# A two-block transformer kernel on one core: three mixer operand pairs packed into one buffer, a 24-slot weight store refilled in another order, and the last gain multiplies on GpSimd

## The chip, the core and the metric

The kernel runs on one core of one Trainium2 chip. A core has five engines with instruction streams of their own: TensorE (PE, matrix products), VectorE (DVE), ScalarE (ACT), GpSimd (POOL) and SyncE (SP), which here does little but start DMA transfers. Data stand in SBUF, products in PSUM, weights in HBM, from which 16 DMA engines fetch them. The metric is the device time of one execution in microseconds (us); lower is better.

## What is computed

A sequence of 256 tokens of width 1024 goes through two blocks of two layers each, all in float32. The first block has a mixer and a mixture of experts in each layer; the second has attention and a convolutional feed-forward network. The parts around the change are these:

```python
# first block, for layer 0 (convolution mixer) and layer 1 (recurrent mixer)
x = layer_norm(ALPHA * x + mixer(x), ln1_g[layer], ln1_b[layer])
f = moe(x, w_router, b_router, moe_w1[layer], moe_w3[layer], moe_w2[layer])
x = layer_norm(ALPHA * x + f, ln2_g[layer], ln2_b[layer])

# both mixers end in a projection
return jnp.einsum("bse,ed->bsd", concatenated_or_gated, w_out)

# each of the 16 experts of a layer
hb = jax.nn.silu(xb @ w1[e]) * (xb @ w3[e])
return hb @ w2[e]

# the end of the second block
x = x + conv_ffn(h, w_up, conv_w, conv_b, w_down)
return rms_norm(x, final_norm_g)        # x * rsqrt(mean(x*x) + eps) * g
```

## The kernel before

**Weights as a stream.** All weights are cut into chunks of 128 x 2048 floats (1 MB). `STREAM` lists them: the input projection of a mixer, its output projection (`ew_out` in layer 0, `ow_out` in layer 1, four chunks each), then 192 expert chunks for a layer (`moe0`, `moe1`; four each of w1, w3 and w2 for each of 16 experts). `sync_load` (L366) starts the loads from SP in the order of `LOAD_ORDER`, which for the first two experts interleaves them: w1 of both, w3 of expert 0, w3 of expert 1, then w2 of both. One load is one DMA of 1 MB, or of 2 MB where `_load_size` gives 2. In this text load 0 is the first expert chunk of a layer, and a 2 MB load has the number of its first chunk.

**Slots.** A chunk lands in one of 24 slots: 0 to 11 are the tile `ring`; 12 to 16 lie in `F` (work space of the mixers and experts), 17 to 20 are the four parts of `early`, 21 and 22 the two halves of `ZX`, and 23 a last part of `F`, used once for each layer. Before it starts a load SP waits until the chunk that was in the slot is used (`released`), and for the first 24 expert loads also until other data are gone from it (`extra_free`). SP works in order, so one wait holds all loads behind it. `FIRST_SLOTS` gives slots to some of the first 24 loads, the rest get the slot that is free first. `GROUPS` names the pairs that a 2 MB load may take; slots 16 and 23 are in no pair.

**The four parts of `early`** have another life in the projections. A dense product is made of three passes on numbers split in a high and a low part: the weights' parts stand in `wh` and `wl` (slots 17 and 18; four pieces of 512 columns, refilled by `scalar_split` on ACT and `vector_split` on DVE), the left operand's in `xh` and `xl` (slots 19 and 20). The output projection of a mixer has four operand pairs q = 0 to 3 (`operand`, L553): pair 0 stands in `F`, pairs 1 to 3 in parts of `xh` and of `xl`. Each takes four weight pieces; `w_used` counts the pieces that PE has used.

**The experts.** `tensor_first_pair` runs experts 0 and 1 together, `moe_tensor` the others one after another. Eight matmul records belong to one chunk (L1431 for w1 of the first pair, L1231 elsewhere). After the last of a chunk `expert_chunk` is raised and its slot is free. From load 128 of a layer on only slots 0 to 11 and 21 are filled, since the others get other work.

**The end.** The last stage `down1` adds its product to `X` (`vector_residual`, L768, four parts: token half h, column half d), takes the squares' sums on ACT (`scalar_rms`, L784), adds them (`vector_rms_sum`, L789), raises to the power -0.5 on POOL (`pool_rstd`, L575), and multiplies by the gain `G` (`gain` in `vector_finish`, L2978, DVE). The product is scaled by the row's factor, on ACT for d = 0 (`scalar_finish`, L3000) and on DVE for d = 1 (`scale`, L2982), and stored by four DMAs (`sync_store`, L3008). The squares are written to `Z`, where the gain's product also goes, so `gain` waits for `square`.

Of the kernel before, what the change touches and what calls it, by code (L numbers as in the profile page):

```python
# [11 lines left out]
ALU = mybir.AluOpType  # L12
# [77 lines left out]
def f32(ap):  # L90
# [26 lines left out]
F_SLOTS, SPLIT_SLOTS, Z_SLOT, XT_SLOT, ONCE_SLOT = range(12, 17), range(17, 21), 21, 22, 23  # L117
FIRST_SLOTS = ([12, 13, 14, 15, XT_SLOT] + [None] * 11 + [16, None, ONCE_SLOT, None, 17, 18, 19, 20],
               [None] * 8 + [16, XT_SLOT, 15, None, None, 14, None, 13, None, 12, ONCE_SLOT, None, 17, 18, 19, 20])
LOAD_ORDER = list(range(len(KIND)))  # L120
# [6 lines left out]
def _load_size(i):  # L127

    return 2 if 40 <= i < 180 else 1

# [88 lines left out]
class Kernel:  # L219
# [311 lines left out]
    def tensor_out_last(self, stage, p, nk):  # L531

        pe, PS = self.pe, self.PS
        pe.wait_ge(self.at("g_lo", stage, nk // 2 - 1))
        for m in range(2):
            x = slice(m * 128, m * 128 + 128)
            for d in range(2):
                for kk in range(2):
# [3 lines left out]
                    pe.wait_ge(self.at("w_lo", n))  # L542
                    t = self.three(PS[:, 2 * m + d, :], (self.xh[:, k % 8, x], self.xl[:, k % 8, x]), (h, l),
                                   False, kk == 1)
# [233 lines left out]
    def scalar_rms(self, stage, src_stage, h):  # L778

        act = self.act  # L780
        for d in range(2):
            c = slice(d * 512, d * 512 + 512)
            act.wait_ge(self.at("resid", src_stage, h, d) if src_stage else self.at("x_final", h))
            act.e.activation(self.Z[:, h, c], self.X[:, h, c], ACT.Square, scale=1.0 / 32,  # L784
                             accum_out=self.sm[:, 430 + 2 * h + d:431 + 2 * h + d]).then_inc(*self.up("square", stage, h, d))
# [201 lines left out]
    def even_scalar(self):  # L987
# [45 lines left out]
        for h in range(2):  # L1033
            for c in (2 * h, 2 * h + 1):
                act.wait_ge(at("ev_scaled", h), at("ev_var"), at("ev_consts", "bh"))
                act.e.activation(v["sq"][:, c, :], v["acc"][:, c, :], ACT.Tanh, scale=v["gh"][:, c:c + 1],
                                 bias=v["bh"][:, c:c + 1]).then_inc(*up("ev_tanh", c))
            self.scalar_split_x("ew_out", 2 + h, self.GT[:, 4 + 2 * h:6 + 2 * h, :], at("ev_gated", 2 * h + 1))
        for n in range(8, 16):
# [964 lines left out]
    def odd_scalar(self):  # L2004
# [404 lines left out]
    def out_scalar(self, stage, p, nk, ready, primed=0):  # L2409
# [14 lines left out]
        self.scalar_rms(stage, stage, 0)
        self.scalar_finish(0)
        self.scalar_rms(stage, stage, 1)
        self.scalar_finish(1)

# [541 lines left out]
    def vector_finish(self, p, nk):  # L2970

        dve, at, up = self.dve, self.at, self.up
        G = self.F[:, 12288:13312]

        def gain(h, d):
            c = slice(d * 512, d * 512 + 512)
            dve.wait_ge((self.s_row, 48), at("resid", "down1", h, d), at("square", "down1", h, d))
            dve.e.tensor_tensor(self.Z[:, h, c], self.X[:, h, c], G[:, c], ALU.mult).then_inc(*up("y_gain", h, d))  # L2978

        def scale(h):  # L2980
            dve.wait_ge(at("rstd", ("down1", h)), at("y_gain", h, 1))
# [3 lines left out]
        self.vector_residual("down1", p, nk, 0, 1.0, self.X)
        self.vector_rms_sum("down1", 0)
        gain(0, 0)
        gain(0, 1)
        self.vector_residual("down1", p, nk, 1, 1.0, self.X, halves=(0,))
        scale(0)  # L2990
        self.vector_residual("down1", p, nk, 1, 1.0, self.X, halves=(1,))
        gain(1, 0)
        self.vector_rms_sum("down1", 1)
        gain(1, 1)
        scale(1)

# [166 lines left out]
```

## Time and profile before

| | us |
|---|---|
| median of 3 runs | 1774.01 |
| lowest and highest | 1773.5, 1775.23 |
| the profiled execution | 1775.5 |
| its span, first to last instruction | 1774.2 |
| PE busy, share of the span | 1709.8, 96% |
| DMA traffic, mean over the span | 307 GB/s |

The page cuts the span in 40 slices of 44 us and gives the DMA rate of each. A window table gives busy time by engine for a stretch, the granted clock, then the DMA engines' share (1.00: all 16 busy) and GB/s. A timeline gives start, duration, engine, line and operation, with like neighbours merged ("x4"); a bracket at its end is the idle time before and what ended it. The view of DMA issues gives for each load its size and the us from issue to landing. The loads have one line, L379, so they are told apart by time.

### The profile page before, as it was taken

The page shows a single profiled execution, that of the slowest core. Times are in us where ns is not written, and L with a number is a line of the kernel's source. Part 1 is how long each engine was busy: PE and PEld are TensorE (multiplying, and loading weights), DVE is VectorE, ACT ScalarE, POOL GpSimd, SP SyncE. Part 2 cuts the span into 40 slices and gives each one's busy share as a digit, 9 for nine tenths or more (in the row PEclk, how much of TensorE's full clock was granted, in tenths as well). Part 3 has the DMA queues.
Part 4 walks back from the last instruction along what each step waited for, and adds up shares of the span by engine and source line. Part 5 has one row for each costly group of instructions (what it writes and reads, how often), then busy time and mean ns, then how long its engine had stood idle before and what let it go on. Part 6 is the DMA issues. An engine that isn't in the chain of part 4 may idle for free.

```text
span 1774.2 us, 23971 instructions
## 1 busy us (share of the span) xinstructions
PE 1709.8 (96%) x9996; PEld 1116.9 (63%) x9996; DVE 791.5 (45%) x1522; ACT 625.2 (35%) x1201; POOL 122.4 (7%) x145
## 2 busy tenths in 40 slices
PE   9999999999989989999999989999999999999998
PEld 8974344433334974444343333887999898789986
DVE  6961111111103782111111012866888677668875
ACT  5541111000002661100000002666666564756664
POOL 0000000000000000000000000131111001401100
PEclk9999999999999999999999999999999999999999
DMA  9769999999999789999999999434555544335550
GB/s 387 314 232 381 387 428 428 428 430 426 426 426 419 284 320 395 423 429 429 429 426 429 425 426 419 174 129 143 177 180 190 190 167 149 137 131 178 179 190 24
DMA packets 55971, 544.88 MB, mean 307 GB/s; under 512 B 6320, under 2 KB 6320, under 8 KB 8368
## 3 DMA queue, kind: packets, MB, share of 16 engines
q1 hardware_dynamic: 55440, 542.14, 75.8%
q8 instruction: 82, 1.34, 0.3%
q10 hardware_dynamic: 416, 1.13, 0.2%
q14 instruction: 33, 0.27, 0.0%
HBM read 542.19 MB, written 1.05 MB: 306 GB/s over the span
## 4 chain that ended last, share of the span: by engine, by line
PE 71%; DMA 16%; DVE 7%; ACT 3%; issue 1%; POOL 1%; SPq 0%; ACTq 0%; DVEq 0%
PE PS L1231 24%; DMA ring<-in_w 16%; PE PS L421 12%; PE PS L423 11%; PE PS L422 11%; PE PS L1213 2%; PE PS L1285 2%; DVE wl L404 2%; PE PS L1431 2%; PE PS L950 1%; PE PS L1247 1%; ACT wh L398 1%; PE PS L1299 1%; PE PS L1404 0%; DVE sm L593 0%
## 5 line engine op out<-in xcount | busy, mean ns | idle before, releaser
L1231 PE MATMUL PS<-ring,F 128*64 128x512 f32 x1992 | 447.4, 598 | 27.5 <-DMA ring<-in_w 23.4
L404 DVE TENSOR_TENSOR wl<-ring,wh 128x512 fp32r<-128x512 f32 x504 | 362.4, 737 | 167.4 <-ACT wh L398 164.9
L398 ACT ACTIVATE wh<-ring 128x512 fp32r<-128x512 f32 x504 | 314.5, 630 | 270.0 <-PE PS L423 251.9
L1231 PEld LDWEIGHTS PS<-ring,F 128*64 128x64 f32 x1992 | 142.3, 138 | 312.0 <-issue 273.6
L421 PE MATMUL PS<-xh,wl 128*128 128x256 f32 x1144 | 329.8, 288 | 2.7 <-DVE wl L404 2.6
L422 PE MATMUL PS<-xl,wh 128*128 128x256 f32 x1144 | 323.6, 283 | 0.0
L423 PE MATMUL PS<-xh,wh 128*128 128x256 f32 x1144 | 323.5, 283 | 0.0
L421 PEld LDWEIGHTS PS<-xh,wl 128*128 128x128 f32 x1144 | 219.2, 192 | 5.8 <-DVE wl L404 2.7
L422 PEld LDWEIGHTS PS<-xl,wh 128*128 128x128 f32 x1144 | 219.3, 192 | 0.7
L423 PEld LDWEIGHTS PS<-xh,wh 128*128 128x128 f32 x1144 | 219.3, 192 | 0.0
L421 PE MATMUL PS<-wh,xl 128*128 128x512 f32 x352 | 142.6, 405 | 6.5 <-DVE xl L566 3.4
L423 PE MATMUL PS<-wh,xh 128*128 128x512 f32 x352 | 137.5, 391 | 0.0
L422 PE MATMUL PS<-wl,xh 128*128 128x512 f32 x352 | 137.3, 390 | 0.0
L1758 DVE COPY F<-PS 64x512 f32<-64x512 f32 x26 | 18.1, 695 | 223.1 <-PE PS L1231 223.1
L1733 DVE SCALAR_TENSOR_TENSOR F<-F,PS 128x512 f32<-128x512 f32 x28 | 19.2, 687 | 203.9 <-ACT F L1548 203.9
L1738 DVE SCALAR_TENSOR_TENSOR F<-F,PS 128x512 f32<-128x512 f32 x28 | 19.2, 687 | 183.1 <-PE PS L1231 183.1
L1231 PE MATMUL PS<-F 128*64 128x512 f32 x384 | 87.1, 594 | 0.4 <-DMA F<-in_w 0.4
L1548 ACT ACTIVATE F<-PS 128x512 f32<-128x512 f32 x28 | 16.7, 597 | 189.3 <-PE PS L1231 189.3
L421 PEld LDWEIGHTS PS<-wh,xl 128*128 128x128 f32 x352 | 66.1, 188 | 26.8 <-DVE xl L566 6.4
L1566 ACT ACTIVATE F<-PS 64x512 f32<-64x512 f32 x26 | 15.3, 590 | 187.6 <-PE PS L1231 187.6
L2643 DVE SCALAR_TENSOR_TENSOR F<-PS,cols,F 128x254 f32<-128x254 f32 (+1 forms) x176 | 76.3, 474 | 1.5
L423 PEld LDWEIGHTS PS<-wh,xh 128*128 128x128 f32 x352 | 66.1, 188 | 14.4
(422 smaller groups left out, 1907.5 us busy)
## 6 DMA issues: line engine op xcount, KB each, us to landing
ring<-in_w SPq DMA_DIRECT2D x100, 2048.0 KB, 25.6
ring<-in_w SPq DMA_DIRECT2D x65, 1024.0 KB, 11.7
ring<-in_ffn_up SPq DMA_DIRECT2D x44, 1024.0 KB, 4.9
early<-in_w SPq DMA_DIRECT2D x16, 2048.0 KB, 26.6
F<-in_w SPq DMA_DIRECT2D x16, 2048.0 KB, 27.9
ring<-in_ffn_down SPq DMA_DIRECT2D x22, 1024.0 KB, 4.9
F<-in_w SPq DMA_DIRECT2D x20, 1024.0 KB, 9.3
ZX<-in_w SPq DMA_DIRECT2D x8, 2048.0 KB, 28.0
```

What stands on the lines that cost most here:

```text
L398: act.e.activation(self.wh[:, p % NPIECE, :], self.piece_source(p), ACT.Copy).then_inc(*self.up("w_hi", p))
L404: dve.e.tensor_tensor(self.wl[:, p % NPIECE, :], self.piece_source(p), f32(self.wh[:, p % NPIECE, :]), ALU.subtract).then_inc(*self.up("w_ ...
L421: e.matmul(out, left[1], right[0], start=first, stop=False)
L422: e.matmul(out, left[0], right[1], start=False, stop=False)
L423: return e.matmul(out, left[0], right[0], start=False, stop=last)
L1213: t = pe.e.matmul(self.PS[:, 6 + half, k4 * 128:k4 * 128 + 128], self.X[:, h, k * 128:k * 128 + 128], v["S"][:, h, :], start=(h == 0), sto ...
L1231: t = pe.e.matmul(PS[64 * half:64 * half + 64, bank, :], lhs(k), weights[:, a:a + 512], start=(k == 0), stop=(k == 7))
L1285: t = pe.e.matmul(self.PS[:, b, :], v["Gt"][:, h, d, :], v["Y"][d], start=(q == 0), stop=False)
L1431: t = pe.e.matmul(PS[64 * half:64 * half + 64, self.first_bank(ex, 0), :], xg[:, k, ex * 64:ex * 64 + 64], weights[:, a:a + 512], start=(k ...
L1733: e.scalar_tensor_tensor(out=self.silu(ex), in0=self.silu(ex), scalar=1.0, in1=PS[:, 4, :], op0=ALU.add, op1=ALU.mult).then_inc(*up("silu" ...
L1738: e.scalar_tensor_tensor(out=v["hh"], in0=self.silu(ex), scalar=0.5, in1=PS[:, 5, :], op0=ALU.mult, op1=ALU.mult).then_inc(*up("hidden", l ...
L2643: t = dve.e.scalar_tensor_tensor(out=dst[:, j, s:256], in0=ps[:, j, 0:256 - s], scalar=cw[:, k, 2 - s:3 - s], in1=dst[:, j, s:256], op0=AL ...
```

## The change

1. **Operand pairs of the mixer outputs.** For `ew_out` and `ow_out` the pairs 1, 2 and 3 all stand in `xl`: high part and low part of a pair side by side, pair 2 in the upper half, pairs 1 and 3 in the lower half. Pair 3 is written after PE has used pair 1 (`w_used`, piece 7). `xh` has no reader after the last piece of the input projection.
2. **One more chunk.** Slot 19 (`xh`) is filled as load 15 in layer 0 and load 12 in layer 1, after that last piece, where it was load 22. The loads that stood there move back by one.
3. **2 MB loads begin with load 44**, not 40. Loads 39 to 43 are single ones, and the pairs of slots for all later loads come in another order.
4. **The end.** Squares are written to a free part of `F`. Three of four gain multiplies are on POOL (`pool_gain`), around `pool_rstd`; DVE keeps the one for h = 1, d = 1. DVE has both residual parts of h = 1 ahead of it, and both scales last. ACT makes all four squares ahead of both `scalar_finish`.

```diff
-FIRST_SLOTS = ([12, 13, 14, 15, XT_SLOT] + [None] * 11 + [16, None, ONCE_SLOT, None, 17, 18, 19, 20],
-               [None] * 8 + [16, XT_SLOT, 15, None, None, 14, None, 13, None, 12, ONCE_SLOT, None, 17, 18, 19, 20])
+FIRST_SLOTS = ([12, 13, 14, 15, XT_SLOT] + [None] * 10 + [19, None, 16, None, ONCE_SLOT, None, 17, 18, 20],
+               [None] * 8 + [16, XT_SLOT, 15, None, 19, None, 14, None, 13, None, 12, ONCE_SLOT, None, 17, 18, 20])
-    return 2 if 40 <= i < 180 else 1
+    return 2 if 44 <= i < 180 else 1
 def extra_free(self, n):
+        if slot == SPLIT_SLOTS[2]:
+            return [self.at("w_used", PIECES[mixer] - 1)]
 def operand(self, stage, q):
+        if stage in MIXER_OUT and q:
+            a = 4 * ((q + 1) % 2)
+            return self.xl[:, a:a + 2, :], self.xl[:, a + 2:a + 4, :]
 def scalar_rms(self, stage, src_stage, h):
+            squares = self.F[:, 8704 + 512 * d:9216 + 512 * d] if stage == "down1" else self.Z[:, h, c]
 def odd_scalar(self):
-        self.scalar_split_x("ow_out", 3, GT[:, 6:8, :], at("od_join", 3))
+        self.scalar_split_x("ow_out", 3, GT[:, 6:8, :], at("od_join", 3), at("w_used", p + 7))
 def out_scalar(...):
+        for h in range(2):
+            self.scalar_rms(stage, stage, h)
+        for h in range(2):
+            self.scalar_finish(h)
 def ffn_pool(self, layer):
+        if layer:
+            for d in range(2):
+                self.pool_gain(0, d)
+        self.pool_rstd(0, (f"down{layer}", 0))
+        if layer:
+            self.pool_gain(1, 0)
+        self.pool_rstd(1, (f"down{layer}", 1))
 def vector_finish(self, p, nk):
+        self.vector_residual("down1", p, nk, 0, 1.0, self.X)
+        self.vector_rms_sum("down1", 0)
+        self.vector_residual("down1", p, nk, 1, 1.0, self.X)
+        dve.wait_ge((self.s_row, 48), at("resid", "down1", 1, 1))
+        dve.e.tensor_tensor(self.Z[:, 1, 512:1024], self.X[:, 1, 512:1024], self.last_gain()[:, 512:1024], ALU.mult
+                            ).then_inc(*up("y_gain_last"))
+        self.vector_rms_sum("down1", 1)
+        for h in range(2):
+            dve.wait_ge(at("rstd", ("down1", h)), at("y_gain_last") if h else at("y_gain", 0, 1))
+            dve.e.tensor_scalar(self.Z[:, h, 512:1024], self.Z[:, h, 512:1024], self.sm[:, 500 + h:501 + h], None,
+                                ALU.mult).then_inc(*up("y_ready1", h))
```

SP, expert loads of layer 0 before, from load 24 to load 49 (128x2048 is 1 MB, 128x4096 is 2 MB; `early` is slots 17 to 20, `F` slots 12 to 16, `ZX` slots 21 and 22):

```order
L379 DMA F<-in_w 128x2048 [waits s_expert_chunk] x4
L379 DMA ZX<-in_w 128x2048 [waits s_expert_chunk]
L379 DMA ring<-in_w 128x2048 [waits s_expert_chunk] x11
L379 DMA early<-in_w 128x4096 [waits s_expert_chunk] x2
L379 DMA F<-in_w 128x4096 [waits s_expert_chunk] x2
L379 DMA ZX<-in_w 128x4096 [waits s_expert_chunk]
```

The same loads now:

```order
L382 DMA F<-in_w 128x2048 [waits s_expert_chunk] x4
L382 DMA ZX<-in_w 128x2048 [waits s_expert_chunk]
L382 DMA ring<-in_w 128x2048 [waits s_expert_chunk] x10
L382 DMA early<-in_w 128x2048 [waits s_expert_chunk]
L382 DMA ring<-in_w 128x2048 [waits s_expert_chunk]
L382 DMA F<-in_w 128x2048 [waits s_expert_chunk]
L382 DMA ZX<-in_w 128x2048 [waits s_expert_chunk]
L382 DMA ring<-in_w 128x2048 [waits s_expert_chunk]
L382 DMA early<-in_w 128x4096 [waits s_expert_chunk]
L382 DMA F<-in_w 128x4096 [waits s_expert_chunk] x2
```

Load 40 was a pair in slots 17 and 18, which hold w2 of expert 1; it is now one chunk in slot 11, which holds the second w2 chunk of expert 0. Loads 41, 42 and 43 follow in slots 16, 21 and 0.

DVE, the end of the program before:

```order
L768 TENSOR_TENSOR X<-X,PS 128x512 [waits s_half_done] x2
L789 TENSOR_SCALAR sm<-sm 128x1 [waits s_square]
L2978 TENSOR_TENSOR ZX<-X,F 128x512 [waits s_resid,s_row]
L2978 TENSOR_TENSOR ZX<-X,F 128x512 [waits s_resid]
L768 TENSOR_TENSOR X<-X,PS 128x512 [waits s_w_used]
L2982 TENSOR_SCALAR ZX<-ZX,sm 128x512 [waits s_y_gain,s_norm_scale]
L768 TENSOR_TENSOR X<-X,PS 128x512 [waits s_w_used]
L2978 TENSOR_TENSOR ZX<-X,F 128x512 [waits s_square,s_resid]
L789 TENSOR_SCALAR sm<-sm 128x1 [waits s_square]
L2978 TENSOR_TENSOR ZX<-X,F 128x512 [waits s_resid]
L2982 TENSOR_SCALAR ZX<-ZX,sm 128x512 [waits s_y_gain,s_norm_scale]
```

and now:

```order
L775 TENSOR_TENSOR X<-X,PS 128x512 [waits s_half_done] x2
L797 TENSOR_SCALAR sm<-sm 128x1 [waits s_square]
L775 TENSOR_TENSOR X<-X,PS 128x512 [waits s_w_used] x2
L2991 TENSOR_TENSOR ZX<-X,F 128x512 [waits s_resid,s_row]
L797 TENSOR_SCALAR sm<-sm 128x1 [waits s_square]
L2996 TENSOR_SCALAR ZX<-ZX,sm 128x512 [waits s_y_gain,s_norm_scale]
L2996 TENSOR_SCALAR ZX<-ZX,sm 128x512 [waits s_y_gain_last,s_norm_scale]
```

Three multiplies and one scale no longer stand ahead of the last residual part and the last sum. On POOL, whose program had ended in two `pool_rstd` in a row, it is now:

```order
L3007 TENSOR_TENSOR ZX<-X,F 128x512 [waits s_resid,s_row]
L3007 TENSOR_TENSOR ZX<-X,F 128x512 [waits s_resid]
L582 TENSOR_TENSOR sm<-sm,mhalf 128x1 [waits s_norm_stats]
L3007 TENSOR_TENSOR ZX<-X,F 128x512 [waits s_resid]
L582 TENSOR_TENSOR sm<-sm,mhalf 128x1 [waits s_norm_stats]
```

so that each power stands behind multiplies.

## Rows read from the trace of the kernel before

**Rows 1.** The page: DMA rate in 40 slices of 44 us.
```profile
GB/s 387 314 232 381 387 428 428 428 430 426 426 426 419 284 320 395 423 429 429 429 426 429 425 426 419 174 129 143 177 180 190 190 167 149 137 131 178 179 190 24
```
**Rows 2.** Windows in layer 0: engines' busy us, clock, DMA share, GB/s.
```profile
150.00:170.00 20.00, 20.00 (x100) 7.73 (x97) 3.42 (x8) 1.68 (x3) 0.00 (x0) 1.00 1.01 422
170.00:180.00 10.00, 10.00 (x66) 5.93 (x64) 1.39 (x2) 1.68 (x3) 0.00 (x0) 1.00 0.76 315
180.00:190.00 10.00, 10.00 (x50) 3.33 (x48) 0.69 (x1) 0.59 (x1) 0.00 (x0) 1.00 0.84 339
210.00:350.00 140.00, 140.00 (x686) 55.79 (x683) 19.13 (x47) 15.35 (x27) 0.00 (x0) 1.00 1.01 428
350.00:548.00 198.00, 183.87 (x849) 69.81 (x847) 18.96 (x37) 16.35 (x28) 0.00 (x0) 0.99 1.01 426
```
**Rows 3.** Timeline of SP: loads 24 to 27, 36 to 39, 40 and 42; layer 1's 24.
```profile
134.97 6.80 SPq L379 DMA_DIRECT2D F<-in_w  x4
...
161.25 6.67 SPq L379 DMA_DIRECT2D ring<-in_w  x4
180.57 3.76 SPq L379 DMA_DIRECT2D early<-in_w  x2
...
675.95 0.33 SPq L379 DMA_DIRECT2D ZX<-in_w  x1
```
**Rows 4.** DMA issues at 99.7, 167.6, 180.6, 197.7, 746.8 us: size, us to landing.
```profile
ring<-in_w SPq DMA_DIRECT2D x1, 1024.0 KB, 4.8
...
ring<-in_w SPq DMA_DIRECT2D x1, 1024.0 KB, 13.0
...
early<-in_w SPq DMA_DIRECT2D x1, 2048.0 KB, 8.6
...
ring<-in_w SPq DMA_DIRECT2D x1, 2048.0 KB, 20.7
...
ZX<-in_w SPq DMA_DIRECT2D x1, 2048.0 KB, 9.0
```
**Rows 5.** Timeline of PE: last reads of xh, first expert products, later ones.
```profile
86.97 0.28 PE L423 MATMUL PS<-xh,wh 128*128 128x256 f32 x1
...
133.00 3.65 PE L1431 MATMUL PS<-F 128*64 128x512 f32 x16
...
167.38 1.89 PE L1231 MATMUL PS<-F 128*64 128x512 f32 x8
...
176.83 7.09 PE L1231 MATMUL PS<-early,F 128*64 128x512 f32 x32
...
202.09 5.37 PE L1231 MATMUL PS<-ring,F 128*64 128x512 f32 x24
...
635.05 0.28 PE L423 MATMUL PS<-xh,wh 128*128 128x256 f32 x1
```
**Rows 6.** Waits of PE from 350 to 562 us: total, times, longest.
```profile
PE PS L1231 <- DMA ring<-in_w: 12.3, 11, 2.5
```
**Rows 7.** Timeline of the last 12 us: DVE, PE, ACT.
```profile
1762.93 0.69 DVE L768 TENSOR_TENSOR X<-X,PS 128x512 f32<-128x512 f32 x1
...
1766.58 0.39 PE L423 MATMUL PS<-wh,xh 128*128 128x512 f32 x1
...
1768.09 0.68 DVE L768 TENSOR_TENSOR X<-X,PS 128x512 f32<-128x512 f32 x1
...
1769.56 0.21 DVE L789 TENSOR_SCALAR sm<-sm 128x1 f32<-128x1 f32 x1 [0.19 <-ACT ZX L784]
...
1770.82 0.72 ACT L3000 ACTIVATE ZX<-ZX,sm 128x512 f32<-128x512 f32 x1 [1.29 <-POOL sm L575]
```
**Rows 8.** A POOL multiply and the DVE beside it; all 18 powers (min/median/max ns).
```profile
1258.77 1.29 POOL L2684 TENSOR_TENSOR F<-F 128x512 f32<-128x512 f32 x1
...
1258.88 1.73 DVE L404 TENSOR_TENSOR wl<-ring,wh 128x512 fp32r<-128x512 f32 x1 [0.68 <-ACT wh L398]
...
L575 POOL TENSOR_TENSOR sm<-sm,mhalf x18: 537/548/932, 119.1 to 1769.9; 128x1 f32<-128x1 f32 x18
```

More of the change, by code:

```diff
@@ L22 @@
 PE_TAPS = 11
+MIXER_OUT = ("ew_out", "ow_out")
 ROUTED = ("ew_out", "ow_out")
@@ L533, in tensor_out_last @@
         pe, PS = self.pe, self.PS
+        xh, xl = self.operand(stage, nk // 2 - 1)
         pe.wait_ge(self.at("g_lo", stage, nk // 2 - 1))
@@ L542, in tensor_out_last @@
                     pe.wait_ge(self.at("w_lo", n))
-                    t = self.three(PS[:, 2 * m + d, :], (self.xh[:, k % 8, x], self.xl[:, k % 8, x]), (h, l),
+                    t = self.three(PS[:, 2 * m + d, :], (xh[:, kk, x], xl[:, kk, x]), (h, l),
                                    False, kk == 1)
@@ L783, in scalar_rms @@
             act.wait_ge(self.at("resid", src_stage, h, d) if src_stage else self.at("x_final", h))
-            act.e.activation(self.Z[:, h, c], self.X[:, h, c], ACT.Square, scale=1.0 / 32,
+            squares = self.F[:, 8704 + 512 * d:9216 + 512 * d] if stage == "down1" else self.Z[:, h, c]
+            act.e.activation(squares, self.X[:, h, c], ACT.Square, scale=1.0 / 32,
                              accum_out=self.sm[:, 430 + 2 * h + d:431 + 2 * h + d]).then_inc(*self.up("square", stage, h, d))
@@ L1037, in even_scalar @@
                                  bias=v["bh"][:, c:c + 1]).then_inc(*up("ev_tanh", c))
-            self.scalar_split_x("ew_out", 2 + h, self.GT[:, 4 + 2 * h:6 + 2 * h, :], at("ev_gated", 2 * h + 1))
+            self.scalar_split_x("ew_out", 2 + h, self.GT[:, 4 + 2 * h:6 + 2 * h, :], at("ev_gated", 2 * h + 1),
+                                *([at("w_used", p + 7)] if h else []))
         for n in range(8, 16):
@@ L2423, in out_scalar @@
             return
[L2424 to L2427, printed above, removed]
+        for h in range(2):
+            self.scalar_rms(stage, stage, h)
+        for h in range(2):
+            self.scalar_finish(h)
     def scalar_split_before(self, p, end):
@@ L2684, in ffn_pool @@
             pool.e.tensor_tensor(acc[i % 2][0], acc[i % 2][0], th[i % 2], ALU.mult).then_inc(*up("gated_unit", layer, i))
-        for h in range(2):
-            self.pool_rstd(h, (f"down{layer}", h))
+        if layer:
[5 more added lines that the diff above has]
+        self.pool_rstd(1, (f"down{layer}", 1))
     def dilated_views(self):
@@ L2972, in vector_finish, with last_gain, pool_gain @@
         dve, at, up = self.dve, self.at, self.up
[L2973 to L2981, printed above, removed]
+        self.vector_residual("down1", p, nk, 0, 1.0, self.X)
[7 more added lines that the diff above has]
+            dve.wait_ge(at("rstd", ("down1", h)), at("y_gain_last") if h else at("y_gain", 0, 1))
             dve.e.tensor_scalar(self.Z[:, h, 512:1024], self.Z[:, h, 512:1024], self.sm[:, 500 + h:501 + h], None,
                                 ALU.mult).then_inc(*up("y_ready1", h))
[L2985 to L2995, printed above, removed]
+    def last_gain(self):
+        return self.F[:, 12288:13312]
+    def pool_gain(self, h, d):
+        c = slice(d * 512, d * 512 + 512)
+        self.pool.wait_ge((self.s_row, 48), self.at("resid", "down1", h, d))
+        self.pool.e.tensor_tensor(self.Z[:, h, c], self.X[:, h, c], self.last_gain()[:, c], ALU.mult).then_inc(
+            *self.up("y_gain", h, d))
     def scalar_finish(self, h):
```

## The prediction, made before the changed kernel ran

> **What bounds the kernel now.** I read the page's DMA rates first [rows 1]. Two plateaus near 426 to 430 GB/s stand out, slices 6 to 13 and 17 to 25, one for each layer's experts. The windows say what is full there: from 210 to 350 us PE is busy all the time and the DMA engines too, from 350 to 548 us the DMA engines are full and PE is busy for 183.87 of 198 us [rows 2]. So PE starts ahead of the stream with full slots, and the stream, which is slower, has caught it up by about 350 us; from there PE waits for landings, 11 times and 12.3 us in all [rows 6]. The end of a layer's experts is therefore the end of its stream: bytes by 426 GB/s, plus each us in which the DMA engines had nothing to do. A load that lands earlier is worth something only if no later load has to wait for a slot all the same. That is the question to ask of edits 2 and 3.
>
> Next I looked for the last such hole in layer 0. The DMA share falls to 0.76 and 0.84 between 170 and 190 us, with 1.01 ahead of it and 1.01 behind [rows 2]. SP shows why: it starts loads 36 to 39 from 161.25 to 167.9 us, then nothing until load 40 at 180.57 [rows 3]. Load 40 is a pair in slots 17 and 18, and PE reads these only from 176.83 us on, 1.77 us for a chunk (7.09 us for 32 records, four chunks) [rows 5], so both are free at 180.5. Load 39 landed at 167.6 + 13.0 = 180.6, so the slowest DMA engine too ran dry, and load 40 landed at 180.6 + 8.6 = 189.2 [rows 4]. A full stream brings 2.10 MB in 4.90 us at 428 GB/s [rows 2]; the hole costs 8.6 - 4.9 = 3.7 us.
>
> **Edit 3 (2 MB loads from load 44).** Load 40 is now one chunk in slot 11, whose chunk (expert 0's second w2) PE has used when its 8 records that begin at 167.38 us end, at about 169.3 [rows 5]. Loads 41 and 42 follow at 1.7 us each, 43 after the first chunk of the group at 176.83, by 178.8. All of them are issued before load 39 has landed, so the queue doesn't run dry. Singles take 1.05 MB / 422 GB/s = 2.48 us [rows 2], so loads 40 to 43 end at 180.6 + 9.9 = 190.5, where before they ended at 189.2 + 4.9 = 194.1. **Gain in layer 0: 3.6 us.**
>
> Does a later load take it back? The tightest is load 52: now in slots 4 and 5, which hold expert 2's first two w2 chunks, used at 202.09 + 2 x 1.8 = 205.7 [rows 5]. On an empty queue it would land 8.6 us after that, at 214.3. The stream reaches it at 190.5 + 5 x 4.9 = 215.0. So it is not late, by 0.7 us. Before, load 52 landed at 197.7 + 20.7 = 218.4 [rows 4]. The gain therefore is 3.4 to 3.6 by the stream and cannot be over 218.4 - 214.3 = 4.1. It passes on to the end of the layer, as PE has 12.3 us of waits to give up [rows 6], and to all that follows.
>
> In layer 1 the same hole isn't there: the DMA rate stays full from slice 17 on, that is from 710 us [rows 1]. There, load 52 needs slots 21 and 22 both before and now, freed at the same PE chunk; it was issued at 746.8 and landed 9.0 us later, at 755.8, where an empty queue would give 755.4 [rows 4]. So layer 1 can gain no more than 0.4 us from edits 2 and 3 together. I take 0.
>
> The windows of singles and doubles, 422 and 428 GB/s [rows 2], show no part of a transfer that is paid in line beyond 0.03 us. A rule of the Trainium skill speaks against edit 3: "DMA: Bandwidth & Descriptors", section "Anatomy of one DMA — SWDGE (gpsimd) path", gives each DMA a fixed part of about 2.0 us beside its bytes. By that page, an estimate with two more transfers for each layer, paid in line, is 8 us more; the trace doesn't agree as long as others are queued (rival D).
>
> **Edits 1 and 2 (xh free early, one more chunk).** `xh` has its last reader at 86.97 us in layer 0 and 635.05 in layer 1 [rows 5]. The new load 15 of layer 0 goes out after load 14 and before the one at 99.7, which was landed 4.8 us later, so it fills an idle DMA engine; it is behind no late wait. It saves nothing: there are 24 slots before and after. Load 24 waits for the first expert chunk to be used, at 134.97 [rows 3] as PE's first products begin at 133.00 [rows 5], and by then all 24 loads are in anyway, one of them 2.5 us sooner. Layer 1 has the same gate at 675.95 [rows 3]. **0 us**, with the caps above as bounds. Pair 3's new wait for `w_used` piece 7 costs nothing on ACT: ACT's own weight splits ahead of it wait for that same piece. DVE's split waits for ACT only. PE's matmul count is the same.
>
> **Edit 4 (the end).** Before, the second residual part of h = 1 began at 1768.09, though PE's last matmul ended at 1766.58 + 0.39 = 1766.97 [rows 7]: DVE was held by multiplies. Now it begins at 1767.0, 1.09 us sooner. From the residual to the last sum it takes 1768.09 to 1769.56, from the sum to the scales 1.26 us [rows 7].
> POOL: first residual done at 1763.62 [rows 7], two multiplies of 1.29 us with 0.1 between [rows 8] to 1766.4, the power, whose median is 0.55 us and most 0.93 [rows 8], to 1767.0, then the multiply for h = 1 to 1768.35.
> DVE: its one multiply comes at 1767.7, amid that. A DVE operation with two SBUF inputs that began 0.11 us after a POOL multiply took 1.73 us and ended 0.55 us after it [rows 8]. So DVE's ends at 1768.9, and the sum begins there, not at 1768.5. With 1.26 us the scales begin at 1770.1, with the power at its short 0.55 at 1769.7. Before: 1770.82. Gain 0.7 to 1.1, I take **0.9 us**. The stores behind keep their spacing. Upper bound 1.5, if DVE isn't held and the power is short (1.09 + 0.38). Lower bound: if each of the three POOL multiplies lost as much to DVE as DVE lost to POOL, 1.73 - 0.69 = 1.04, the second power would end at 1768.35 + 3.1 + 0.55 = 1772.0, a loss of 1.2.
>
> **Sum.** The profiled execution took 1775.5 with a span of 1774.2; the median is 1774.01, and I subtract from that: 1774.0 - 3.6 - 0 - 0.9 = **1769.5 us**. The span should be 1769.7.
>
> **Rivals.**
> A. The extra chunk is carried through as a head start in both layers, 2.5 us each, because the slowest DMA engine binds and it alone was still busy when load 24 came. For: that the load whose bytes take 2.5 us landed 4.8 us after issue [rows 4] leaves room for a start that overlaps better. Against: the caps of load 52, 4.1 and 0.4 us. Time: 1769.5 - 5.0 = 1764.5.
> B. The hole only moves. With the pairs in another order the queue runs dry at load 52 or later, and layer 0 gains nothing. For: a margin of 0.7 us, on a latency seen once for a pair on an empty queue. Against: as soon as it holds, later loads are issued further ahead, since PE is the faster. Time: 1774.0 - 0.9 = 1773.1.
> C. Slower: restart. The DMA engines now stand idle for 2.5 us longer ahead of load 24, in both layers, all 16 of them. If a restart from fully dry costs as the one at 180 did (3.7 us for hole and start together), once more in each layer, it is 1774.0 - 4.5 + 7.4 = 1776.9. It decides if the landing of loads 24 and 25 is later than before by over 2.3 us a layer. Against: single loads on a dry queue landed in 4.8 us [rows 4], 2.3 over their bytes, the same before and now.
> D. Slower: the fixed part is paid in line. By rows it is 4.8 - 2.5 = 2.3 us for a single; two more transfers a layer make 9.2 us: 1778.7. Against: 422 beside 428 GB/s.
>
> **How the numbers follow.** Forecast 0.75, A 0.07, B 0.11, C 0.05, D 0.02. The forecast's own range takes the caps (4.1 + 0.4 + 1.5 = 6.0: 1768.0) and on the other side the losing end (3.4 - 1.2 = 2.2: 1771.8). With B at 1773.1 in it and some scatter of the runs (1773.5 to 1775.2) on the low side, 1767.0 to 1773.2 holds over 0.8. A measurement tells about 0.2% or 3.5 us from no change, so faster means under 1770.5. The forecast lies there in about 5 of 6 of its cases, 0.63, with A 0.70; the rest of it and B make 0.23 the same; C and D 0.07 slower.
>
> **What would show it.** Right: DMA share near 1.0 from 140 us to the end of layer 0's experts, load 40 landing at about 183 and load 52 at 215; the last landing and all stages behind 3.6 us earlier; the first expert products at 131.8 us as before, layer 1's expert stretch as long as before; in the last 12 us a DVE multiply of 1.2 us or more, and scales that begin 2.7 to 3.1 us after PE's last matmul, where it was 3.85. Wrong: a hole near 205 us (B), loads 24 and 25 later (C), landings of singles over 2.6 us apart (D), load 24 itself issued earlier or layer 1 shorter by over 0.4 us (A).

## The result and the profile after

| | us |
|---|---|
| before, median of 7 runs | 1774.23 |
| after, median of 7 runs | 1768.88 (1768.28 to 1770.26) |
| ratio | 0.997, 95% interval 0.9961 to 0.9979 |
| the profiled execution after, its span | 1770.26, 1769.0 |

The changed kernel is 5.35 us faster, where 4.5 were forecast, and 1769.5 was forecast for 1768.88. The profiled execution is the slowest of the seven. The loads' line L379 is L382 now, L423 is L426, and L1231 is L1240.

The page of the changed kernel has its two plateaus where they were [rows 1], and the windows of layer 0 (columns as in [rows 2]) show the hole at 180 us filled:

```profile
GB/s 389 315 238 378 420 429 427 427 429 427 425 424 420 275 345 375 420 430 427 429 427 427 423 426 420 182 125 143 180 180 189 191 167 147 140 132 170 188 189 26
```
```profile
170.00:180.00 10.00, 10.00 (x66) 5.88 (x64) 1.39 (x2) 1.68 (x3) 0.00 (x0) 1.00 1.01 419
180.00:190.00 10.00, 10.00 (x50) 3.43 (x48) 0.69 (x1) 0.59 (x1) 0.00 (x0) 1.00 1.03 432
203.00:206.00 3.00, 3.00 (x16) 1.01 (x14) 0.00 (x0) 0.00 (x0) 0.00 (x0) 1.00 0.99 426
206.00:209.00 3.00, 3.00 (x16) 1.00 (x14) 0.12 (x1) 0.12 (x1) 0.00 (x0) 1.00 0.95 311
210.00:350.00 140.00, 140.00 (x687) 56.03 (x684) 19.12 (x47) 15.35 (x27) 0.00 (x0) 1.00 1.01 428
```

315 and 339 GB/s have become 419 and 432. There is a new, smaller dip, 311 GB/s from 206 to 209 us. SP's timeline of the changed kernel, layer 0 (loads 24 to 27, 29 to 38, 40, 43, 44, then 50 and 52) and load 24 of layer 1:

```profile
134.63 6.80 SPq L382 DMA_DIRECT2D F<-in_w  x4
...
145.86 20.00 SPq L382 DMA_DIRECT2D ring<-in_w  x10
...
168.97 0.33 SPq L382 DMA_DIRECT2D ring<-in_w  x1
...
178.47 0.33 SPq L382 DMA_DIRECT2D ring<-in_w  x1
181.95 0.33 SPq L382 DMA_DIRECT2D early<-in_w  x1
...
197.40 8.42 SPq L382 DMA_DIRECT2D ring<-in_w  x2
...
672.72 0.33 SPq L382 DMA_DIRECT2D ZX<-in_w  x1
```

DMA issues of the changed kernel at 89.8 (the extra chunk), 169.0 (load 40), 205.5 (load 52) and 743.5 us (load 52 of layer 1), size and us to landing:

```profile
early<-in_w SPq DMA_DIRECT2D x1, 1024.0 KB, 6.9
...
ring<-in_w SPq DMA_DIRECT2D x1, 1024.0 KB, 12.6
...
ring<-in_w SPq DMA_DIRECT2D x1, 2048.0 KB, 8.6
...
ZX<-in_w SPq DMA_DIRECT2D x1, 2048.0 KB, 8.9
```

Load 40 landed at 169.0 + 12.6 = 181.6 (183 forecast), load 52 at 205.5 + 8.6 = 214.1 (215.0 forecast, 218.4 before).

The last 12 us of the changed kernel, timelines of PE, DVE, POOL and ACT:

```profile
1762.55 0.39 PE L426 MATMUL PS<-wh,xh 128*128 128x512 f32 x1
...
1762.98 0.69 DVE L775 TENSOR_TENSOR X<-X,PS 128x512 f32<-128x512 f32 x1 [0.43 <-PE PS L426]
1763.77 0.84 DVE L2991 TENSOR_TENSOR ZX<-X,F 128x512 f32<-128x512 f32 x1
1764.53 0.20 DVE L797 TENSOR_SCALAR sm<-sm 128x1 f32<-128x1 f32 x1
...
1764.23 0.19 ACT L792 ACTIVATION_READ_ACCUMULATOR F<-X 128x1 f32 x1
...
1759.73 2.59 POOL L3007 TENSOR_TENSOR ZX<-X,F 128x512 f32<-128x512 f32 x2 [56.46 <-DVE X L775]
1762.27 0.55 POOL L582 TENSOR_TENSOR sm<-sm,mhalf 128x1 f32<-128x1 f32 x1
1762.79 1.27 POOL L3007 TENSOR_TENSOR ZX<-X,F 128x512 f32<-128x512 f32 x1
1764.81 0.72 POOL L582 TENSOR_TENSOR sm<-sm,mhalf 128x1 f32<-128x1 f32 x1 [0.75 <-DVE sm L797]
...
1765.57 0.72 ACT L3013 ACTIVATE ZX<-ZX,sm 128x512 f32<-128x512 f32 x1 [0.54 <-POOL sm L582]
```

The last scales begin 1765.57 - 1762.94 = 2.63 us after the end of PE's last matmul, where it was 3.85 [rows 7].

**Where the 5.2 us of span went.** The same instruction in both traces, by [rows 3, 7] and the rows above: load 24 of layer 0 is issued 0.34 us earlier (chance: nothing ahead of it is quicker by design), load 24 of layer 1 3.23 earlier, the last matmul 4.03, the last scales 5.25. So 2.9 us fell in layer 0's stretch, 0.8 between layer 1's load 24 and the last matmul, and 1.2 in the end. The 0.8 is not the stream's: layer 1's last load landed only 2.8 us earlier than before, so that in this execution its stream took 0.5 us longer (419.8 us from the issue of load 24 to the last landing, for 419.3; the other traces with the extra chunk and 2 MB loads have 418.0 to 419.1), and 1.3 us fell between that landing and the last matmul. This part is a slow stretch of PE in the trace of before (last section).

### The profile page after: what moved, and what is told of

Its sections match the earlier page's. It is cut to its first block, busy times and chain, and to the rows that moved or that the text cites. A ratio compares the mean times of both kernels' runs of the same rounds, so it can differ in the third digit from the quotient of the medians.

```text
span 1769.0 us, 23968 instructions
## 1 busy us (share of the span) xinstructions
PE 1709.5 (97%) x9996; PEld 1116.6 (63%) x9996; DVE 789.8 (45%) x1519; ACT 625.1 (35%) x1201; POOL 125.6 (7%) x148
## 4 chain that ended last, share of the span: by engine, by line
PE 69%; DMA 18%; DVE 7%; ACT 3%; issue 1%; POOL 1%; SPq 0%; ACTq 0%; DVEq 0%
PE PS L1240 22%; DMA ring<-in_w 18%; PE PS L424 12%; PE PS L426 11%; PE PS L425 11%; PE PS L1222 2%; DVE wl L407 2%; PE PS L1440 2%; PE PS L1294 2%; PE PS L958 1%; PE PS L1256 1%; ACT wh L401 1%; PE PS L1308 1%; PE PS L1413 1%; DVE sm L600 0%
## 5 line engine op out<-in xcount | busy, mean ns | idle before, releaser
L1240 PE MATMUL PS<-ring,F 128*64 128x512 f32 x1984 | 446.4, 597 | 25.4 <-DMA ring<-in_w 20.0
L1240 PEld LDWEIGHTS PS<-ring,F 128*64 128x64 f32 x1984 | 140.6, 137 | 308.1 <-issue 268.3
L426 PE MATMUL PS<-xh,wh 128*128 128x256 f32 x1144 | 323.5, 283 | 0.0
L425 PEld LDWEIGHTS PS<-xl,wh 128*128 128x128 f32 x1144 | 219.3, 192 | 0.6
L426 PEld LDWEIGHTS PS<-xh,wh 128*128 128x128 f32 x1144 | 219.3, 192 | 0.0
L426 PE MATMUL PS<-wh,xh 128*128 128x512 f32 x304 | 118.7, 391 | 0.0
L425 PE MATMUL PS<-wl,xh 128*128 128x512 f32 x304 | 118.6, 390 | 0.0
L1240 PE MATMUL PS<-F 128*64 128x512 f32 x384 | 87.1, 593 | 0.0
L1240 PE MATMUL PS<-early,F 128*64 128x512 f32 x336 | 76.1, 594 | 0.0
```

The costliest lines, as they stand in the source:

```text
L425: e.matmul(out, left[0], right[1], start=False, stop=False)
L426: return e.matmul(out, left[0], right[0], start=False, stop=last)
L1240: t = pe.e.matmul(PS[64 * half:64 * half + 64, bank, :], lhs(k), weights[:, a:a + 512], start=(k == 0), stop=(k == 7))
```

## The experiments

All are timed beside the kernel before, whose median was 1774.2 to 1774.3 each time. For the stream I read one mark from each profile: the time from the issue of load 24, which is where PE has used the layer's first chunk, to the landing of load 100. It leaves out what happened ahead of the layer.

| kernel | extra chunk | 2 MB from | time, us | layer 0 mark | layer 1 mark |
|---|---|---|---|---|---|
| before | no | 40 | 1774.2 | 201.0 | 198.1 |
| end4 | no | 40 | 1772.90 | 201.1 | 197.5 |
| load44 | no | 44 | 1770.73 | 196.9 | 197.5 |
| noextra | no | 44 | 1770.07 | 197.1 | 198.3 |
| end4_52 | no | 52 | 1769.55 | 197.1 | 198.6 |
| slot19 | yes | 40 | 1776.01 | 203.8 | 196.9 |
| stream123 | yes | 44 | 1769.95 | 197.1 | 197.0 |
| after | yes | 44 | 1768.88 | 197.5 | 197.3 |
| extra (the same) | yes | 44 | 1769.31 | 197.2 | 196.7 |
| sumfirst | yes | 44 | 1769.03 | 196.9 | 196.8 |
| after52 | yes | 52 | 1768.73 | 197.3 | 197.2 |
| swap52 | yes | 44 | 1771.94 | 200.5 | 196.8 |
| singles | yes | none | 1777.66 | 196.1 | 196.7 |

before, load44, slot19 and stream123 have the old end, the others the new one. One mark varies by 0.6 to 1.1 us between kernels that should have the same, so only its groups are compared.

Outside the two streams and the end the traces are alike. Between the last expert landing of layer 0 and the issue of load 24 in layer 1 lie 118.5 to 118.6 us in all thirteen, with the operand pairs of edit 1 or without. Between the last landing of layer 1 and the end of the last matmul lie 670.5 to 670.6, but for before (671.7) and end4_52 (671.3). From there to the end of the span it is 7.25 us with the old end and 6.1 with the new one (6.2 in sumfirst).

### The parts by themselves

**load44.** Edit 3 alone:

```diff
-    return 2 if 40 <= i < 180 else 1
+    return 2 if 44 <= i < 180 else 1
```

> Edit 3 alone: the kernel before with 2 MB loads from load 44 instead of 40. Theory 1 (the forecast: the hole at 180 us in layer 0 is the whole gain of the stream): no hole, load 40 issued near 169 and landed at 183, load 52 issued at 205.8 and landed near 215.1 instead of 218.5, about 3.5 us less in all, 1770.7. Theory 2 (the extra chunk of edit 2 also puts the stream 1.9 us ahead behind load 24, and load 52 cuts this off): there is no extra chunk here, so the same 3.4 us, and load 25 lands 10.8 us after load 24 was issued, as before; 1770.8. Rival B (the hole only moves to load 52): load 52 lands at 218 and the time is 1774.

1770.73 us, ratio 0.9979 (0.9970 to 0.9988). Window from 180 to 190 us, and the pair issued at 205.6 us:

```profile
180.00:190.00 10.00, 10.00 (x50) 3.38 (x48) 0.69 (x1) 0.59 (x1) 0.00 (x0) 1.00 1.01 424
```
```profile
ring<-in_w SPq DMA_DIRECT2D x1, 2048.0 KB, 8.6
```

The hole is gone and the time fell by 3.6 us. But load 52 landed at 214.2, as in the changed kernel, and load 25 came 8.7 us after the issue of load 24, without an extra chunk. So theory 2's evidence falls here: the 10.8 us for load 25 in the trace of before was one slow landing of that execution. The kernel end4 has the same old stream and shows 8.6.

**slot19.** Edits 1 and 2 alone, with the old end:

```diff
-FIRST_SLOTS = ([12, 13, 14, 15, XT_SLOT] + [None] * 11 + [16, None, ONCE_SLOT, None, 17, 18, 19, 20],
+FIRST_SLOTS = ([12, 13, 14, 15, XT_SLOT] + [None] * 10 + [19, None, 16, None, ONCE_SLOT, None, 17, 18, 20],
...
     return 2 if 40 <= i < 180 else 1
```

> Edits 1 and 2 alone: operand pairs in one buffer and the extra chunk, with 2 MB loads from load 40 and the old end. Theory 1 (the forecast: these edits are worth 0): 1774.2, hole at 180 us as before. Theory 2: loads 25 to 39 land 1.5 to 2 us earlier, but the hole takes it all back, and more: slots 17 and 18 now hold expert 1's second and third w2 chunk, so the pair for load 40 comes free one chunk (1.7 us) later, near 182.2, and lands at 190.8 instead of 189.2; layer 0 is 1.6 us longer, layer 1 gains at most 0.4 by the same cap at load 52; 1775.6. Rival A (a head start carried through in both layers) would give 1769.

1776.01 us, ratio 1.0009 (1.0000 to 1.0018): slower by 1.7 us. Windows, then SP's timeline (loads 39 and 40), then the pair of load 40:

```profile
170.00:180.00 10.00, 10.00 (x64) 5.86 (x62) 1.39 (x2) 1.68 (x3) 0.00 (x0) 1.00 0.79 329
180.00:190.00 10.00, 10.00 (x50) 3.33 (x48) 0.69 (x1) 0.59 (x1) 0.00 (x0) 1.00 0.66 246
```
```profile
167.81 15.03 SPq L382 DMA_DIRECT2D early<-in_w  x2
```
```profile
early<-in_w SPq DMA_DIRECT2D x1, 2048.0 KB, 8.6
```

The second of the two issues began at 182.51 and ended at 167.81 + 15.03 = 182.84; the pair landed at 191.1 where it was 189.2. By moving the loads behind it back one place the extra chunk had put later chunks into slots 17 and 18 (the second and third w2 chunk of expert 1, where the first and second had been), and the pair waited for them. By the marks layer 0 lost 2.8 us and layer 1 gained 1.2. Not all of the 2.8 is the pair's: at load 50 it is 1.7 us. Load 52 took 0.3 us over the full rate and load 82 1.0 us, though issued 26 us ahead of the landing in front of it. Such late landings with a full queue, of 0.5 to 1.6 us, come two to six times in every trace.

**stream123.** Edits 1 to 3, the old end (the slots of slot19, with 44).

> Edits 1, 2 and 3 together, with the old end. Theory 1: as edit 3 alone, 1770.6, load 52 landing near 215.1. Theory 2: load 25 lands 9.0 us after load 24's issue instead of 10.8, load 52 is then ready before its slots are and is issued onto an almost empty queue at 205.8, landing 8.6 us later at 214.4; 4.1 us in layer 0 and 0.1 to 0.4 in layer 1, 1769.9. Against edit 3 alone the landing of load 52 tells the two apart by 0.7 us, the total hardly.

1769.95 us, ratio 0.9976 (0.9967 to 0.9986). Load 52 landed at 213.4, 0.8 us earlier than in load44, but its layer 0 mark is no better than load44's (197.1 and 196.9): load 54, next behind it, landed 5.9 us after load 52, at 219.3, where load44 has 219.1. So neither theory's landing came, and the head start was gone one load later. In layer 1 its mark is 0.5 better.

**end4.** Edit 4 alone, on the kernel before:

```diff
-        gain(1, 0)
         self.vector_rms_sum("down1", 1)
-        gain(1, 1)
-        scale(1)
...
+            for d in range(2):
+                self.pool_gain(0, d)
```

> Edit 4 alone: the new end behind the old stream. Forecast: 0.9 us less, 1773.3, last scales 2.7 to 3.1 us after the end of the last matmul where it was 3.85. As the trace of the whole change reads: 1.2 us less, 1773.0, scales 2.6 us after it, the one DVE multiply 0.8 us long, ending 0.55 us after POOL's multiply. If the end were worth nothing by itself, 1774.2.

1772.9 us, ratio 0.9993 (0.9984 to 1.0002). PE, then DVE at the end:

```profile
1765.35 0.39 PE L423 MATMUL PS<-wh,xh 128*128 128x512 f32 x1
...
1766.57 0.84 DVE L2983 TENSOR_TENSOR ZX<-X,F 128x512 f32<-128x512 f32 x1
...
1768.37 0.48 DVE L2988 TENSOR_SCALAR ZX<-ZX,sm 128x512 f32<-128x512 f32 x1 [0.45 <-POOL sm L575]
```

1768.37 - 1765.74 = 2.63 us again, 1.2 less than before. The times say 1.4, with zero just inside the interval; the trace is what carries this.

### Is there still a hole at load 52, and what does the extra chunk bring?

**after52.** The changed kernel with its size rule at 52 (`return 2 if 52 <= i < 180 else 1`).

> The changed kernel with 2 MB loads from load 52 instead of 44. Load 52 then takes slots 2 and 3, free 6 us earlier, so nothing has to wait at 205.5 us. Theory 1 (no hole is left in the stream): four more transfers in each layer, 0.08 us each, 1769.5. Theory 2 (the windows of the changed kernel show 311 GB/s at 206 to 209 us and 344 at 743.7 to 746.7, which by 426 GB/s is 0.8 and 0.6 us of lost stream in front of load 52): these go, 1.4 less 0.6 for the transfers, 1768.1, and both windows show 420 or more. Theory 3 (the extra chunk is carried as a head start of 1 us or more in each layer and load 52 had hidden it): 1767.0.

1768.73 us, ratio 0.9969 (0.9957 to 0.9981). The window that had 311 GB/s:

```profile
206.00:209.00 3.00, 3.00 (x18) 1.00 (x16) 0.00 (x0) 0.00 (x0) 0.00 (x0) 1.00 1.07 456
```

The dip is gone as theory 2 said. The time lies between theories 1 and 2 and settles neither: it is 0.15 us less than 1768.88 and 0.6 less than the second timing of the changed kernel (extra, 1769.31), and neither can be told from none. Theory 3 is out: no execution took less than 1768.09. In layer 0 load 54 landed 84.9 us after the issue of load 24, no earlier than the 84.2 to 84.7 of the kernels with 2 MB loads from 44, so nothing of the 0.8 us that bytes over 426 GB/s give is seen there.

**end4_52.** The same without the extra chunk (old slots and operands).

> The same without edits 1 and 2: the old operands and slots, the new end, 2 MB loads from load 52. Theory 1 and 2 (the extra chunk is worth nothing, since load 24 waits for PE in both): the same as the kernel with it but for the holes that it had, 1769.0 at most 0.5 off its partner. Theory 3: 1 us or more in each layer slower than with the extra chunk, 1769.5 or more beside 1767.0.

1769.55 us, ratio 0.9973 (0.9964 to 0.9982), 0.8 us above its partner.

**noextra** and **extra.** The changed kernel without edits 1 and 2, beside the changed kernel itself.

> The changed kernel without edits 1 and 2: old operands and slots, 2 MB loads from load 44, the new end; to be compared with the changed kernel itself, timed beside it. Theory 1 (the extra chunk is worth 0, as forecast, since load 24 waits for PE either way): no difference, 1768.9 to 1769.2 for both. Theory 2 (without it load 23 is still on the way when load 24 is issued, 1.2 us in layer 0 and 2.1 us in layer 1 by the trace of the kernel before, and the slowest DMA engine passes that on until load 52's slots bind): 0.3 to 0.5 us in each layer, 0.8 in all, 1769.7 beside 1768.9.

> The changed kernel once more, beside the one without the extra chunk on the same chip. Both theories: 1768.9; load 23 lands before load 24 is issued or within 0.2 us of it, in both layers.

1770.07 (0.9965 to 0.9986) and 1769.31 us (0.9956 to 0.9980): again 0.8 apart. Theory 2 has the total right, but not the split. Three pairs, load44 with stream123, end4_52 with after52 and this one, differ by 0.78, 0.82 and 0.76, each less than its own intervals resolve. The marks say where it lies. Layer 0, with no hole at 180: 197.0 without the chunk (three kernels), 197.2 with it (five). Layer 1: 198.0 without (five), 197.0 with it (seven, singles left out); at the landing of load 178 there are 0.7 us of this left, 390.6 and 389.9, and single kernels of the two groups overlap there. Read at other loads from 30 to 178 the means differ by 0.3 to 1.1. So the chunk is worth nothing in layer 0 and about 0.7 us of stream in layer 1. Where the two groups part is in SP's timeline of layer 1, loads 23 and 24, each kernel with the us to landing of the two. Without the extra chunk:

```profile
665.62 0.33 SPq L379 DMA_DIRECT2D early<-in_w  x1
671.88 0.33 SPq L379 DMA_DIRECT2D ZX<-in_w  x1
```
```profile
early<-in_w SPq DMA_DIRECT2D x1, 1024.0 KB, 8.5
...
ZX<-in_w SPq DMA_DIRECT2D x1, 1024.0 KB, 7.7
```

With it:

```profile
667.04 0.33 SPq L382 DMA_DIRECT2D early<-in_w  x1
673.31 0.33 SPq L382 DMA_DIRECT2D ZX<-in_w  x1
```
```profile
early<-in_w SPq DMA_DIRECT2D x1, 1024.0 KB, 5.9
...
ZX<-in_w SPq DMA_DIRECT2D x1, 1024.0 KB, 4.7
```

Without it load 23 landed at 674.1, 2.2 us after load 24 had been issued; with it at 672.9, 0.4 us before. That holds for every kernel of the table: 2.0 to 2.3 us after it without the chunk, between 0.4 before and 0.7 after it with the chunk. In layer 0 it is 0.7 to 1.2 us after without it, and there load 24 landed 4.7 to 5.0 us after its issue with the chunk and without. In layer 1 that took 4.7 to 5.2 us with it; without it 7.6 to 7.8 in three kernels (before, noextra, end4_52), whose marks are 198.1 to 198.6, and 6.3 and 4.9 in end4 and load44, whose marks are 197.5. The trace has 16 semaphore steps for each load, and the last is the landing. In noextra's layer 1 fifteen of load 23's were in by 672.8 and the last came at 674.2; of load 24's fifteen by 676.7, the last at 679.6. So the lateness was that of a last part, carried from one load to the next. That this is the chunk's 0.8 us is the likely reading, but not shown: no run moved load 23 alone, and load44 had the same lateness and passed on little of it.

**swap52.** The changed kernel with the slots of two loads exchanged:

```diff
+            elif (layer, i) in ((0, 52), (0, 54)):
+                group = (6, 7) if i == 52 else (4, 5)
             elif i < 128:
```

> The changed kernel with the slots of loads 52 and 54 of layer 0 exchanged: load 52 now waits for slots 6 and 7, whose last chunk PE has used 3.4 us later. It asks how much room load 52 has before it costs. Theory 1 (the forecast's cap: a pair on a dry queue lands 8.6 us after its issue, and load 52 stands at that cap already): issue at 208.9, landing 217.5, 3.4 us later than now, and the whole time with it, 1772.3. Theory 2 (the slowest DMA engine, which sets the landings, is behind the others by more than 2 us and goes on while they are dry, so that a late issue is partly free): landing near 215.5, 1770.5.

1771.94 us, ratio 0.9985 (0.9976 to 0.9994): slower than the changed kernel by 2.6 to 3.1 us. Windows in layer 0, and the pair of load 52, issued at 208.93; last the pair of layer 1 issued at 745.8, which the edit leaves alone:

```profile
206.00:209.00 3.00, 3.00 (x16) 1.00 (x14) 0.11 (x1) 0.11 (x1) 0.00 (x0) 1.00 0.21 87
209.00:212.00 3.00, 3.00 (x16) 1.00 (x14) 0.59 (x1) 0.48 (x1) 0.00 (x0) 1.00 0.67 218
```
```profile
ring<-in_w SPq DMA_DIRECT2D x1, 2048.0 KB, 8.6
...
ZX<-in_w SPq DMA_DIRECT2D x1, 2048.0 KB, 7.7
```

208.9 + 8.6 = 217.5, theory 1 to a tenth, and the mark is 3.3 us longer. The pair at 208.9 was issued 0.4 us ahead of the landing of load 50 and cost the stream 3.4 us. The pair of layer 1 was issued 2.8 us ahead of the landing in front of it, landed 4.9 us behind that, and cost nothing.

That is no rule for layer 0. In the thirteen traces 17 pairs were issued 2.8 to 4.2 us ahead of the landing in front. The six with 3.7 or more lost nothing. Of the eleven with less, five lost nothing (four of them in layer 1) and six lost 0.3 to 1.0 us, most at the load behind: in layer 0 load 54 landed 5.4 to 5.9 us after load 52 in extra, noextra, sumfirst and stream123 (load 52 issued 3.0 to 3.3 ahead), 5.1 in the changed kernel (3.6) and 4.9 in load44 (3.7). So load 52 of the changed kernel stands at the edge of its room.

### The size of a load, and the end

**singles.** The changed kernel with `return 1`.

> The changed kernel with 1 MB loads throughout. Forecast's theory (the fixed part of a transfer is hidden while others are queued): 68 more transfers in each layer at 2 x 2.49 - 4.90 = 0.08 us, 10.9 us, less 1.4 for the holes at load 52: 1778. Rival D (2.3 us a transfer, paid in line): over 2000. If transfers of 1 MB ran at the same 428 GB/s as those of 2 MB: 1767.5.

1777.66 us, ratio 1.0020 (1.0010 to 1.0029), as the forecast's theory says. The window from 220 to 340 us:

```profile
220.00:340.00 120.00, 120.00 (x598) 49.19 (x596) 15.95 (x39) 12.57 (x22) 0.00 (x0) 1.00 1.01 423
```

423 GB/s beside 428 is all that 1 MB loads lose: 8.8 us over 136 more transfers, 0.065 us each. Rival D is out.

**sumfirst.** The changed kernel with one operation moved:

```diff
+        self.vector_rms_sum("down1", 1)
         dve.wait_ge((self.s_row, 48), at("resid", "down1", 1, 1))
...
-        self.vector_rms_sum("down1", 1)
```

> The changed kernel with DVE's one multiply behind the last sum instead of ahead of it. The sum then waits for ACT alone and begins 0.1 us earlier; the multiply begins 0.7 us after the end of POOL's and takes 0.69 instead of 0.84, but runs beside the last power. Theory 1 (POOL's power is slowed by a DVE operation with two SBUF inputs beside it: 0.93 where it is 0.72 behind the sum now): the last scales begin 0.1 us later than now, 2.7 to 2.75 us after the end of the last matmul, 1769.0. Theory 2 (DVE held in front of the sum is what costs): 0.1 to 0.2 us earlier, 2.45 to 2.5 us.

1769.03 us, ratio 0.9972 (0.9960 to 0.9983), no difference that can be told. DVE, then POOL:

```profile
1763.57 0.21 DVE L797 TENSOR_SCALAR sm<-sm 128x1 f32<-128x1 f32 x1 [0.79 <-ACT F L792]
1763.70 0.68 DVE L2992 TENSOR_TENSOR ZX<-X,F 128x512 f32<-128x512 f32 x1
...
1763.87 0.95 POOL L582 TENSOR_TENSOR sm<-sm,mhalf 128x1 f32<-128x1 f32 x1 [0.68 <-DVE sm L797]
```

The multiply takes 0.68 with no multiply of POOL beside it, and the power 0.95 beside it. The scales began 2.79 us after the last matmul, 0.16 later than in the changed kernel: theory 1. By the traces, multiply ahead of the sum is the better order.

## Why the prediction was right, and where it was off

**What bounds it.** Right: the plateaus stayed, PE still ran out of landed chunks well ahead of the layer's end, and what the stream gained in layer 0 passed on to all behind it. The place was off: PE's first wait for a load in layer 0 is at 370.4 us before and at 396.5 now, not at 350.

**Edit 3.** The mechanism and place were right and load44 shows it alone: 3.6 us timed, 3.6 forecast; the marks say 3.9 (201.0 to 197.1). The small miss is the margin of load 52. The forecast took the stream's place from one execution, in which load 39 landed 45.6 us after the issue of load 24; the four other profiles without the extra chunk show 44.5 to 45.2. Counted from the issue of load 24, load 52 landed 0.5 to 0.9 us sooner in the three of them with the new sizes than the forecast's 215.0 - 135.0 = 80.0.

**The cap.** This step took a number for a rule. "Issue plus 8.6" was read at a hole, where the queue was fully dry, and used as the earliest landing of any pair. A pair issued while its predecessor has 2.8 us to go lands 7.7 us after its issue. In layer 1 this is kept, which is how its mark could fall by 1.1 us where the forecast allowed 0.4. In layer 0 it is not: load 54 landed 13.4 to 13.8 us after load 52's issue in all seven kernels with 2 MB loads from 44, where the cap and one load at full rate give 8.6 + 4.9 = 13.5. There the cap held, one load later than it was put. Whether the late issue makes it so is open, since load 54 came no earlier where load 52 was issued 8 us earlier (after52, end4_52). With the queue dry the 8.6 is exact (swap52).

**Edits 1 and 2.** The term was 0, and the runs give 0.8 us in time, three times over, and 0.3 to 1.1 in layer 1, 0.7 at its end. The step that failed is "by then all 24 loads are in anyway". They were not: load 23 landed 2.1 us after load 24 was issued in layer 1. That could have been read before the change: issue and landing of load 23 were in the trace, and the step argued from load 24's gate only. Right was that load 24 itself doesn't move and that edit 1, with ACT's new wait, is free: load 24 of layer 0 is issued at 134.7 to 135.1 us without it and at 134.6 to 135.2 with it (136.3 once), and the stretch from layer 0's last landing to load 24 in layer 1 is 118.5 to 118.6 us in every trace. That the price comes through load 23's last part is likely, not shown (noextra).

**What the parts owe each other.** The forecast gave edits 1 and 2 a term of 0 and did not ask what they do with the old sizes. They cost 1.7 us without edit 3 (slot19), by a pair that then waits for a later chunk. Its parts' times don't add either: -3.6, +1.7 and -1.4 make -3.3, the whole is -5.35.

**Edit 4.** 1.2 us by the traces of after and end4, for 0.9. The rule from [rows 8] held: DVE's multiply ended 0.55 us after POOL's (1764.61 and 1764.06). Two sizes were off: POOL's multiplies have no gap of 0.1 between them (2.59 for two), so that POOL was done 0.26 us sooner than the forecast's chain, counted from the first residual; and the last power took 0.72, between the 0.55 and the 0.93 that the two ends of the forecast count. The forecast "a multiply of 1.2 us or more" was wrong: it began later in POOL's and took 0.84. So the last sum began 1.59 us after the last matmul (1764.53 - 1762.94), where the forecast has 1768.9 - 1767.0 = 1.9: this is the 0.3 us that edit 4 gave beyond its term. The sum was hardly held by the multiply. ACT's last square was in at 1764.42, and with no multiply ahead of it (sumfirst) the sum began after 1.51 us.

**Rivals.** A and B each had a grain: layer 1's head start is about 0.7 us, not 2.5, and the hole that moved to load 52 is one of 0.3 us, 0.5 to 1.0 in four other kernels. C: restarts after load 24 were no dearer with the extra chunk (load 25 7.8 to 9.3 us after load 24's issue with it, 8.0 to 10.9 without). D: 0.065 us and not 2.3. The Trainium skill, "DMA: Bandwidth & Descriptors", section "Anatomy of one DMA — SWDGE (gpsimd) path", gives about 2.0 us of fixed cost for each DMA, on the path started from GpSimd. It isn't seen in line here, where SP starts the loads with others queued.

**Signs.** The DMA share was a poor sign to name: it stayed at 0.95 in the window with 311 GB/s. The GB/s column showed it. And 131.8 for the first expert products was their preparation's time in that trace; the products themselves begin at 133.00 [rows 5], and 132.67 now.

## What to carry to other kernels

When a stream of loads sets the end of a stage, list for each load its issue, its predecessor's landing and its own landing: a 2 MB load issued 3.7 us or more ahead of its predecessor's landing here cost nothing (six cases), one issued 2.8 to 3.6 ahead nothing in five cases and 0.3 to 1.0 us in six, one issued at it or 0.4 ahead 3.4 to 3.8. A pair needs both of its slots, so check any change in the order of slots for the pair that now holds a later chunk; make loads single until the pairs' slots are far behind the reader. An extra buffer is worth at most what is still in flight at the next gate.

## What the runs showed beyond that

**A dip in bytes is not a loss of its size.** From 206 to 209 us the changed kernel moved 311 GB/s, by bytes a loss of 0.8 us, yet the landings of loads 50, 52 and 54 were 5.0 and 5.1 us apart where 4.9 is the full rate: 0.3 us lost. The 16 semaphore steps of each load show how both can be. Load 50's came from 206.4 to 209.1 us, the middle one at 207.0; load 52's from 212.4 to 214.1, the middle one at 212.7. The middle steps are 5.7 us apart, 0.8 over the full rate, the last ones 5.0. So the parts that were done early stood dry, while the last part, which makes the landing, still had work. The trace doesn't name the DMA engine of a step.

**TensorE's clock after a wait.** In the kernel before, after waits of 2.50 and 2.12 us for a load, PE took 5.35 and 5.33 us for 16 records that take 3.65 elsewhere, and the granted clock of the windows was 0.72, so part of each was spent at 1.2 GHz. After a wait of 1.25 us, at 1051.22, they took 3.65. Windows, then PE's timeline:

```profile
401.00:407.00 6.00, 5.96 (x18) 1.90 (x19) 0.56 (x1) 0.00 (x0) 0.00 (x0) 0.72 0.98 418
...
1057.00:1063.00 6.00, 6.00 (x18) 1.91 (x19) 0.63 (x1) 0.00 (x0) 0.00 (x0) 0.72 1.00 423
```
```profile
1051.22 3.65 PE L1231 MATMUL PS<-ring,F 128*64 128x512 f32 x16 [1.25 <-DMA ring<-in_w]
1056.99 5.33 PE L1231 MATMUL PS<-ring,F 128*64 128x512 f32 x16 [2.12 <-DMA ring<-in_w]
```

After the second one PE no longer waited for a load in that layer, so in that execution PE and not the stream ended it.
